# A two-layer decoder trunk on one core: the sigmoid gates spread thinner, two token tiles split earlier, and the scale and shift done by half rows

## The reference, cut to what matters

```python
def even_layer(x, pos, ...):
    h = x @ w_in
    cq, ckv, k_rope, g_mla, u, g_s5 = _split(h, EVEN_SPLITS)
    o_mla = mla_attention(cq, ckv, k_rope, pos, ...) * silu(g_mla)       # 8 heads, causal, 1024 x 512
    o_s5 = s5_layer(u, ...) * silu(g_s5)                                 # 1024 x 256
    return concatenate([o_mla, o_s5], axis=-1) @ w_out                   # 768 -> 1024

# the end of s5_layer: y = gelu(y); y = y * sigmoid(y @ w_glu + b_glu)
# after the layer:     x = layer_norm(alpha * x + y, ln_g, ln_b)
# layer_norm:          (x - mean) * rsqrt(var + eps) * g + b, over the 1024 of a token
```

## Time and profile before

| what | value |
|---|---|
| median of 3 runs | 937.69 us |
| the 3 runs | 937.26, 937.69, 940.99 us |
| the profiled execution's own time | 938.81 us |
| its span in the trace | 937.1 us |
| PE busy | 882.4 us, 94% of the span |
| DVE busy | 481.9 us, 51% |
| ACT busy | 283.4 us, 30% |
| POOL busy | 251.7 us, 27% |
| mean granted clock of TensorE | 0.973 |

### The profile page before, as it was taken

The page is one execution under the profiler, slowest core; times in us unless marked ns, Lnnn a source line. Parts: engine busy times, 40 slices in busy tenths (PEclk is TensorE's granted clock), DMA queues, the critical chain, the costliest instruction groups (busy, mean ns, idle before and its releaser), DMA issues. The chain is left out here.

```text
span 937.1 us, 12044 instructions
## 1 busy us (share of the span) xinstructions
PE 882.4 (94%) x4456; PEld 716.0 (76%) x4456; DVE 481.9 (51%) x805; ACT 283.4 (30%) x554; POOL 251.7 (27%) x259
## 2 busy tenths in 40 slices
PE   7999999987889999988999899999999999999995
PEld 6888776755558877776876688888888888888884
DVE  6988789468776655436883364100000025654453
ACT  6252425542223433322221654102020226221120
POOL 2000002422211080003643633033403343142243
PEclk9999999997699999999999899999999999999998
DMA  9011256200010020032225120021101232012111
GB/s 333 19 28 35 74 79 128 71 0 1 1 45 1 2 68 1 1 91 68 101 103 155 40 63 13 2 89 45 34 23 45 90 123 90 24 67 70 45 45 68
DMA packets 35050, 55.80 MB, mean 60 GB/s; under 512 B 7744, under 2 KB 21312, under 8 KB 34976
## 3 DMA queue, kind: packets, MB, share of 16 engines
q1 hardware_dynamic: 34992, 55.03, 19.6%
HBM read 43.94 MB, written 9.44 MB: 57 GB/s over the span
## 5 line engine op out<-in xcount | busy, mean ns | idle before, releaser
L1592 DVE SCALAR_TENSOR_TENSOR w_out_lo<-w_out_raw,vecs,w_out_hi 128x1024 fp32r<-128x1024 f32 x8 | 10.3, 1285 | 162.1 <-ACT w_out_hi L1180 161.9
L1883 PEld LDWEIGHTS psum<-V,probT 128*128 128x128 f32 x576 | 71.9, 198 | 18.5 <-issue 8.5
L1883 PE MATMUL psum<-V,probT 128*128 128x64 f32 x576 | 77.1, 281 | 5.2 <-DVE probT L602 4.9
L1746 PE MATMUL psum<-kT,qTt 96*128 96x512 f32 (+3 forms) x192 | 75.7, 505 | 1.2 <-DVE YT L619 1.2
L1093 ACT ACTIVATE prob<-psum,negmax 128x128 f32<-128x128 f32 (+7 forms) x64 | 47.4, 741 | 93.8 <-DVE negmax L1472 70.2
L1472 DVE TENSOR_REDUCE negmax<-psum 128x1 f32<-128x128 f32 (+7 forms) x64 | 48.5, 758 | 43.3 <-PE psum L1750 42.1
L602 DVE COPY probT<-psum 128x512 f32<-128x512 f32 (+3 forms) x64 | 37.9, 592 | 27.6 <-PE psum L1668 26.0
L931 POOL TENSOR_TENSOR zn<-zn,ln_gb 128x1024 f32<-128x1024 f32 x8 | 21.8, 2726 | 110.0 <-DVE zn L1255 110.0
L1659 PE MATMUL psum<-x1T_hi,wqk_hi 128*128 128x512 f32 x128 | 50.9, 398 | 0.0
L1659 PE MATMUL psum<-x1T_hi,wqk_lo 128*128 128x512 f32 x128 | 50.8, 397 | 0.0
L1659 PE MATMUL psum<-x1T_lo,wqk_hi 128*128 128x512 f32 x128 | 50.8, 397 | 0.0
(11 more groups left out here) (360 smaller groups left out, 2062.0 us busy)
## 6 DMA issues: line engine op xcount, KB each, us to landing
wqk_raw<-odd_w_in_dram SPq DMA_DIRECT2D x8, 512.0 KB, 5.4
x_res<-x_dram SPq DMA_DIRECT2D x8, 512.0 KB, 3.7
x_scratch<-zn SPq DMA_DIRECT2D x8, 512.0 KB, 2.7
wv_raw<-odd_w_in_dram SPq DMA_DIRECT2D x16, 256.0 KB, 2.6
wg_raw<-odd_w_in_dram SPq DMA_DIRECT2D x16, 256.0 KB, 2.7
w_out_raw<-odd_w_out_dram SPq DMA_DIRECT2D x4, 1024.0 KB, 5.0
V<-x_scratch SPq DMA_DIRECT2D x8, 512.0 KB, 4.0
out_dram<-SG SPq DMA_DIRECT2D x8, 512.0 KB, 2.9
```

The source lines that it names most:

```text
L1592: step(vec.scalar_tensor_tensor(w_out1[2][:, k, :], w_out1[0][:, k, :], gla_c[:, 4 + k % 2:5 + k % 2], w_out1[1][:, k, :].bitcast(F32), AL ...
L1746: mm = pe.matmul(psum[:, slot + part, 0:c1 - c0], qTt[:, i % 2, h, :], kT[:, h, c0:c1], start=True, stop=not diag, skip_group_check=diag)
L1883: mm = pe.matmul(bank("o", i)[:, h * VD:(h + 1) * VD], lhsT, rhs, start=(k == 0), stop=(k == len(pairs) - 1))
```

## The change

It changes four things and adds no arithmetic.

1. The 16 gates stand behind every second head from 24 to 54, which is rows 3 to 6, instead of behind each head of rows 1 and 2.
2. SP loads slice 0 of `w_out0` and the first head's `wqk` before it waits for the sixteenth gate, and slices 4 and 5 after it; POOL splits slice 0 first.
3. Tiles 0 and 1 of the output projection are split inside attention: the rounded parts behind heads 58 and 60 on ScalarE, the rests behind heads 59 and 61 on VectorE.
4. The scale and shift is done by half rows, in four instructions for two, and `x1_set` counts halves. TensorE turns one half tile behind each column half of the projection: the second half of tile `i - 2` behind `("z0", i, 0)`, and the first half of tile `i - 1` behind `("z0", i, 1)`.

```diff
@@ PSUM banks of the output stage
         for i in range(NT):
             if i:
                 ring("z0", i, 0)
+                if i >= 2:
+                    ring("x1T", i - 2, 1)
                 ring("z0", i, 1)
-            if i:
                 ring("x1T", i - 1, 0)
-                ring("x1T", i - 1, 1)
+        ring("x1T", NT - 2, 1)
@@ SP
             sp.wait_ge(s5_states_set, 4)
+            plan.filled(sp, ("q", NT - 1, 1))
+            sp.wait_ge(q_turned, NT)
+            w_out0_load(0, 1)
+            wqk_load(0)
             sp.wait_ge(s5_out_set, 16)
             for k in range(4, 6):
-                w_out0_load(k, 1)
-            plan.filled(sp, ("q", NT - 1, 1))
-            sp.wait_ge(q_turned, NT)
-            w_out0_load(0, 2)
-            wqk_load(0)
+                w_out0_load(k, 2)
...
-                    sp.wait_ge(x1_set, i - 1)
+                    sp.wait_ge(x1_set, 2 * (i - 1))
@@ POOL
+            w_out0_split_slice(0, 1, 16)
             for k in range(4, 6):
-                w_out0_split_slice(k, 1, 32)
-            w_out0_split_slice(0, 2, 16)
+                w_out0_split_slice(k, 2, 32)
...
                 pool.wait_ge(centred, i + 1)
-                z = zn[:, i % 2, :]
-                step(pool.tensor_tensor(z, z, ln_gb[:, 0, :], ALU.mult))
-                step(pool.tensor_tensor(z, z, ln_gb[:, 1, :], ALU.add), x1_set)
+                for half in range(2):
+                    s = slice(half * 512, (half + 1) * 512)
+                    step(pool.tensor_tensor(zn[:, i % 2, s], zn[:, i % 2, s], ln_gb[:, 0, s], ALU.mult))
+                    step(pool.tensor_tensor(zn[:, i % 2, s], zn[:, i % 2, s], ln_gb[:, 1, s], ALU.add), x1_set)
@@ ScalarE, attention
-                elif what == "z0":
-                    mix_hi_tile(0)
                 elif what == "pt":
...
+                    if n in (58, 60):
+                        mix_hi_tile((n - 58) // 2)
...
-            mix_hi_tile(1)
@@ VectorE, attention
                     copy_probs(vec, step, number, first, blocks)
-                    if 8 <= n < 24:
-                        sigmoid_gate(n - 8)
+                    if 24 <= n < 56 and n % 2 == 0:
+                        sigmoid_gate((n - 24) // 2)
+                    if n in (59, 61):
+                        mix_lo_tile((n - 59) // 2)
...
-                elif what == "z0":
-                    mix_lo_tile(0)
...
-            mix_lo_tile(1)
@@ TensorE, output stage
             for i in range(1, NT):
-                output(i)
-                x1_turned(i - 1)
+                output(i, 0)
+                if i >= 2:
+                    x1_turned(i - 2, 1)
+                output(i, 1)
+                x1_turned(i - 1, 0)
+            x1_turned(NT - 2, 1)
```

More of the change, by code:

```diff
@@ L503, in hybrid_trunk, with x1_halves @@
                 ring("z0", i, 0)
+                if i >= 2:
+                    ring("x1T", i - 2, 1)
                 ring("z0", i, 1)
-            if i:
                 ring("x1T", i - 1, 0)
-                ring("x1T", i - 1, 1)
+        ring("x1T", NT - 2, 1)
+        def x1_halves(i):
+            if i == NT:
+                return [(NT - 1, 0), (NT - 1, 1)]
+            return [(j, half) for j, half in ((i - 2, 1), (i - 1, 0)) if j >= 0] + ([(i - 1, 1)] if i == NT - 1 else [])
         plan.give(("gk", 0), 0)
@@ L785, in _ @@
                 if i >= 2:
-                    sp.wait_ge(x1_set, i - 1)
+                    sp.wait_ge(x1_set, 2 * (i - 1))
                     sp.dma_start(x1_rows[(i - 2) * P:(i - 1) * P, :], zn[:, i % 2, :]).then_inc(x1_stored[i % 2], 16)
             for i in range(NT - 2, NT):
-                sp.wait_ge(x1_set, i + 1)
+                sp.wait_ge(x1_set, 2 * (i + 1))
                 sp.dma_start(x1_rows[i * P:(i + 1) * P, :], zn[:, i % 2, :]).then_inc(x1_stored[i % 2], 16)
@@ L1140, in _ @@
                     low_hi(0)
[L1141 to L1146, removed]
+                for j, half in x1_halves(i):
+                    plan.filled(act, ("x1T", j, half))
+                    step(act.activation(x1T_hi[:, 4 * half:4 * half + 4, j * P:(j + 1) * P],
+                                        bank("x1T", j, half).rearrange("p (k t) -> p k t", k=4), ACT.Copy),
+                         x1_hi_set)
             low_hi(1)
@@ L1553, in _ @@
                     mix_lo_tile(i + 2)
[L1554 to L1559, removed]
+                for j, half in x1_halves(i):
+                    vec.wait_ge(x1_hi_set, 2 * j + half + 1)
+                    at_ = (slice(None), slice(4 * half, 4 * half + 4), slice(j * P, (j + 1) * P))
+                    step.frees(vec.tensor_tensor(x1T_lo[at_], bank("x1T", j, half).rearrange("p (k t) -> p k t", k=4),
+                                                 x1T_hi[at_].bitcast(F32), ALU.subtract), ("x1T", j, half))
             low_lo(1)
@@ L1838, in _, with output, x1_turned @@
                           [(w_glu[:, k, m * P:(m + 1) * P], YT[:, k, half * 512:(half + 1) * 512]) for k in range(2)])
-            def output(i):
-                if i == 0:
+            def output(i, n):
+                if i == 0 and n == 0:
                     pe.wait_ge(w_out0_split, MIX // P)
[L1843 to L1855, removed]
+                if n == 0:
+                    pe.wait_ge(mix_split, i + 1)
+                plan.claim(pe, ("z0", i, n))
+                ts, cs = slice(i * P, (i + 1) * P), slice(n * 512, (n + 1) * 512)
+                group(("z0", i, n), bank("z0", i, n),
+                      split_pairs([((mix_hi[i % 2][:, k, :], OT_lo[:, k, ts] if k < 4 else gs5_lo[:, k - 4, ts]),
+                                    (w_out0_hi[:, k, cs], w_out0_lo[k][:, cs])) for k in range(6)]))
+            def x1_turned(i, half):
+                pe.wait_ge(x1_set, 2 * i + half + 1)
+                turned(("x1T", i, half), [(zn[:, i % 2, k * P:(k + 1) * P], P)
+                                          for k in range(4 * half, 4 * half + 4)])
             for what, n in attention_steps():
@@ L1861, in _ @@
                 elif what == "z0":
-                    output(n)
+                    output(n, 0)
+                    output(n, 1)
                 elif what == "qT":
@@ L1924, in _ @@
             queries_keys(0)
-            x1_turned(NT - 1)
+            for half in range(2):
+                x1_turned(NT - 1, half)
             for i in range(NT // 2, NT):
```

## The result

The changed kernel takes 907.2 us in the median of four runs (906.12 to 909.96). The ratio to the kernel before is 0.9663, interval 0.963 to 0.9697, so it is 3.4% faster. The forecast was 906 us, range 897 to 920. Single disturbed executions are left out of them; the profiled one of e1 was such a one, so that kernel's profile is e12.

The account below looks back on a forecast made before the run. VectorE was taken to bound rows 1 and 2, with waits at the seam and VectorE's pace in the output stage. Attention 20.8 plus output stage 11.1 gave 31.9 us off 938.8, 906.9, forecast as 906 us against the median; range 897 to 920.

Parts of the forecast that it names:

- VectorE was the bound of rows 1 and 2: Attention rows 1 and 2: VectorE, busy 22.73 of 25.62 and 26.05 of 32.33 us, makes PE wait.
- What the gates cost in their new places: Attention rows 3 to 6: 2.4 us of waits in row 3, 2.5 us given up in rows 4 to 6.
- The waits at the starts of rows: Rows 1 and 2: PE still waits for norm and second qT copy, 1.8 and 1.0 us.
- the 5 named as a sign: Attention: the waits for qT copies should sum to under 5 us.
- The clock: Attention: 1.5 us kept for one fall of PE's clock behind grouped waits.
- which would have shown me wrong: Attention rows 3 to 6: a fall of the clock there was named as refuting the prediction.
- The seam: Attention's end: early splits remove waits of 3.17 and 2.04 us and slow matmuls, 8.9 us; 1.6 us wait stays.
- VectorE's cycle sets the pace, at 8.6 it no longer does.: Steady output stage: VectorE's 9.71 us a tile exceeds PE's 9.13; half-length POOL operations give 2.1 us.
- Weight slices: Rows 5 to 7: loads and splits after gate 16 fit into some 24 us to spare, so nothing waits.
- New rows bound by VectorE: Rival, chance 0.17: rows 3 and 4 turn VectorE-bound, clock falls, 10 to 20 us return; 920 us.
- A new wait in place of the old: Rival, chance 0.10: in the output stage half turns wait for POOL's halves, only attention gains; 908 us.
- Slower: Rival, chance 0.03: in rows 3 to 6 each gate delays PE by its length, 25 us, and the clock falls.

Follow-up runs that it names:

- e1: Kernel before with only the gates' new places and the later load of weight slices 4 and 5: 915.75 us, ratio 0.9746.
- e12: The kernel of e1 run again for a profile: 915.51 us.
- e7: Changed kernel with a gate at each head of rows 3 and 4 instead of every second head of rows 3 to 6: 917.08 us, ratio 0.9785.
- e6: Changed kernel with each gate's three instructions replaced by a copy of one column: 903.18 us, ratio 0.9636.
- e13: e8 with the second qT copy of each row made by ScalarE instead of VectorE: 901.11 us, ratio 0.9596.
- e5: Changed kernel with POOL's scale and shift on whole rows again, TensorE still turning by halves: 911.82 us, ratio 0.9712.
- e8: Changed kernel with gates at heads 2 to 7 of rows 4 and 5 and 2 to 5 of row 6: 906.26 us, ratio 0.9658.
- e14: e8 with the last OT copied behind the first layer norm and ScalarE's root table loaded ahead: 901.02 us, ratio 0.9592.
- e4: Kernel before with only POOL's scale and shift cut into four operations of 512 columns, tiles turned whole: 936.77 us, ratio 0.9996.
- e2: Kernel before with only tiles 0 and 1 split inside attention: 933.91 us, ratio 0.9945.
- e15: The edits of e13 and e14 together, gates in rows 4 to 6: 897.38 us, ratio 0.9553.

## Why the prediction was right

- **VectorE was the bound of rows 1 and 2.** Right: e1 and e12 give the whole gain of attention alone (22.6 us; 20.8 + 1.5 = 22.3 were foreseen without the clock's fall), and e7 makes the same picture in rows 3 and 4. Row 2 was foreseen at 19.4 us and lasts 19.6, row 3 at 22.9 and lasts 23.2, row 4 at 28.1 and lasts 27.8.
- **What the gates cost in their new places.** 3.5 us by e6. I had counted 2.4 of waits in row 3, most of it the gates', 1.5 in row 4 and 1.0 in rows 5 to 7. They are 2.2, 1.2 and 0.1: in rows 5 and 6 nearly all of a gate fits into VectorE's idle time.
- **The waits at the starts of rows.** Waits of 0.3 + 1.4 us in row 1 and 0.9 in row 2 (1.8 and 1.0 foreseen). e13 shows the cause of the 1.4 and the 0.9, since the copy taken from VectorE removes them; the 0.3 stays. All waits for `qT` copies sum to 3.8 us, under the 5 named as a sign.
- **The clock.** One fall at 1.5 us was kept; in the profile it is 1.7 us behind row 1's wait. That this profile has it is luck: in e5 to e8, e12 and e14, with the same wait of 1.4 us, it did not happen there. Nor did the clock fall in rows 3 to 6, which would have shown me wrong.
- **The seam.** The waits of 3.17 and 2.04 us and their slow matmuls are gone, as counted. The wait for the first turned half was foreseen at 1.6 us and is 2.20, a mis-sized term: POOL's first operation took 1.69 us next to VectorE, not 1.35. e14 shows that this wait hangs on the `OT` copy and the table load together.
- **"VectorE's cycle sets the pace, at 8.6 it no longer does."** The size was right (9.71 to 9.13 us a tile), and e5 shows the cycle at 9.76. The reason was incomplete: e4 has the shorter cycle and a pace of 9.46, since a tile turned whole also waits for POOL, which is done 9.58 us behind the tile's last matmul and wanted at 9.05. I had worked out such a number only for the turned halves, and at 8.7 us it was too short: I took four operations at 5.4 us, and from start to end they take 5.90. The halves had room for it, so the sum came out.
- **Weight slices.** Nothing waited for them: no profile here shows a wait of the projection for a weight slice.
- **The rivals.** New rows bound by VectorE: half true of row 3, which lost 2.2 us to its gates. A new wait in place of the old: true of e2 and e4, where only a part of the change is made, not of the whole, whose steady part runs at 9.13 us a tile and not at 9.71. "Slower" had each gate delay PE by its length, 25 us; it is 3.5.
- **The number.** 906 us was forecast and 907.2 measured, 31.9 us of gain against 31.8 in the profiles. That is closer than the terms are: row 1 with its clock gave 0.6 us less than foreseen, the seam and output stage 0.7 less, rows 5 to 7 0.9 more, and 0.7 came from the start, which the change doesn't touch. They cancel.

## What to carry to other kernels

Work that is off the critical path belongs where its engine has idle time by the stretch, not by the whole: the 25 us of gates cost 3.5 in rows where they left VectorE at or below PE's time, and had stretched rows 1 to 3 by about their own length (82.9 us before, 59.1 in e12). Place such work behind the instructions that the bounding engine waits for at the start of each round rather than ahead of them; row 4 of e8 speaks for it. When a stage runs at a pace slower than its bounding engine, look for a cycle (one engine's sum) and for a latency (the chain until a result is wanted back) separately. Here the cycle alone held the pace at 9.76 us a tile (e5), the latency alone at 9.46 (e4), and only without both was it PE's 9.13. And an edit that shortens the cycle can lengthen the latency: four short operations took 0.5 us more than two long ones.

## What the runs showed of the hardware

Whether the clock falls behind a wait of PE of 1.4 to 2.2 us was not settled by the wait's length. These rows stand at the same place in two kernels, the changed kernel first and then e8, each behind a wait of 1.39 us:

```profile
209.26 2.90 PE L1663 MATMUL psum<-w_uq,cT 128*128 128x384 f32 x4 [1.39 <-DVE qTt L1472]
```

```profile
208.81 1.56 PE L1665 MATMUL psum<-w_uq,cT 128*128 128x384 f32 x4 [1.39 <-DVE qTt L1472]
```

The first are at 1.2 GHz, the second at 2.4. Of the seven profiles with this wait (the changed kernel, e5 to e8, e12 and e14) only the changed kernel's shows the fall. In the same way the wait of 2.20 us for the first turned half was followed by a full-speed stretch in the changed kernel and e6, and took 1.6 us more in e7 and e8. In e13 the wait was 2.56 us and the clock stayed; behind waits of 3.77 us in e4 and 4.36 in e2 and e5 it fell. So part of the spread between kernels of one design, up to 3.3 us for these two places together, is such a fall or its absence; that e13 to e15 are better also because they leave it fewer waits is a guess. What decides it stays open.

A VectorE instruction with two operands in SBUF, blocked by a POOL operation, ends about 0.3 us after that operation (455.16 for 454.89 in the earlier trace rows): `gs_lo` took 2.50 us beside operations of 1024 columns, 1.39 beside 512, 0.42 alone. That agrees with what the Trainium skill states on the page "SBUF — State Buffer", section "Who interferes with whom": such an instruction contends with a GpSimd instruction that reads SBUF, since the two share ports, and the sharing is an exclusive lock.
